# Opening of the first (gated linear attention) mixer: order of its first projections, their PSUM banks, and the zero matmuls

## What is computed

```python
def gla_mixer(h, w_in, w_gk2, b_gk, g_norm, w_out):
    proj = h @ w_in
    q, k, v, r, lr = jnp.split(proj, [GLA_DK, 2 * GLA_DK, 2 * GLA_DK + GLA_DV, 2 * GLA_DK + 2 * GLA_DV], axis=-1)
    gk = jax.nn.log_sigmoid((lr @ w_gk2 + b_gk).astype(f32)) / GLA_GATE_NORMALIZER
    ...
    b = jnp.cumsum(gc, axis=2)
    b_mid = b[:, :, GLA_CHUNK // 2:GLA_CHUNK // 2 + 1]
    q_in = qc * jnp.exp(b - b_mid)
    k_in = kc * jnp.exp(b_mid - b)
    causal = jnp.tril(jnp.ones((GLA_CHUNK, GLA_CHUNK), dtype=bool))
    scores = jnp.einsum('bcihd,bcjhd->bchij', q_in, k_in)
    ...
    o = rmsnorm(o, g_norm.reshape(GLA_HEADS, GLA_HV)).reshape(bsz, t_len, GLA_DV)
    o = o.astype(h.dtype) * jax.nn.silu(r)
    return o @ w_out
```

## Time and profile before

| | us |
|---|---|
| median of 3 runs | 1169.73 |
| lowest and highest | 1167.99, 1170.42 |
| the profiled execution, its own time | 1166.21 |
| its span in the trace | 1164.5 |
| TensorE busy in the span | 1111.0 (95%) |
| VectorE busy | 733.4 (63%) |
| ScalarE busy | 631.9 (54%) |
| TensorE's share of the chain that ended last | 88% |

### The profile page before, as it was taken

One profiled execution on the slowest core, in us unless ns is written; L12 is line 12 of the kernel. 1 busy time (PEld: TensorE's weight loads), 2 busy tenths in 40 slices (PEclk: granted clock), 3 DMA queues, 4 the chain that ended last, 5 costly groups with the idle time before them and its releaser, 6 DMA issues.

```text
span 1164.5 us, 16442 instructions
## 1 busy us (share of the span) xinstructions
PE 1111.0 (95%) x5868; PEld 947.5 (81%) x5868; DVE 733.4 (63%) x1170; ACT 631.9 (54%) x984; POOL 54.1 (5%) x81
## 2 busy tenths in 40 slices
PE   6899999969989999999999997999999989999997
PEld 5788888868968888888888885889999977888886
DVE  4555545656587555457655545598999978655553
ACT  6444444665367444447544444576776776544443
POOL 3000000000000000000000000221122100000000
PEclk9899999989999999999999999899999989999999
DMA  7756554444446565554756534484555424765530
GB/s 249 253 181 211 172 173 129 127 145 145 145 142 226 192 215 176 171 195 129 246 185 210 173 100 148 134 283 148 160 160 164 145 72 159 258 216 180 172 116 37
DMA packets 162877, 199.24 MB, mean 171 GB/s; under 512 B 6372, under 2 KB 145856, under 8 KB 162832
## 3 DMA queue, kind: packets, MB, share of 16 engines
q1 hardware_dynamic: 160144, 190.34, 50.4%
q0 software_dynamic: 2384, 7.72, 1.9%
q10 hardware_dynamic: 304, 0.61, 0.1%
HBM read 197.56 MB, written 1.08 MB: 171 GB/s over the span
## 4 chain that ended last, share of the span: by engine, by line
PE 88%; DVE 6%; ACT 3%; issue 1%; DMA 1%; SPq 0%; DVEq 0%; ACTq 0%
PE ps L1414 41%; PE ps L1433 25%; PE ps L1466 8%; PE ps L1476 6%; PE ps L1425 2%; PE ps L1775 1%; DVE ws L918 1%; DVE ws L1000 1%; PE ps L1456 1%; ACT ws L530 1%; DMA raw<-in_ffn_w_down 1%; PE ps L1584 1%; DVE xT L990 1%; DVE xres L966 0%; DVE ca L1191 0%
## 5 line engine op out<-in xcount | busy, mean ns | idle before, releaser
L1414 PE MATMUL ps<-ws,xT 128*128 128x512 f32 x2160 | 502.4, 391 | 6.2 <-DVE ws L1000 6.2
L1414 PEld LDWEIGHTS ps<-ws,xT 128*128 128x128 f32 x2160 | 404.9, 188 | 93.7 <-DVE ws L1000 8.0
L1433 PE MATMUL ps<-ws,hT 128*128 128x512 f32 x1344 | 335.2, 400 | 4.0 <-DVE hT L1291 3.9
L1433 PEld LDWEIGHTS ps<-ws,hT 128*128 128x128 f32 x1344 | 251.5, 191 | 57.5 <-issue 5.9
L1000 DVE TENSOR_TENSOR ws<-raw,ws 128x1024 fp32r<-128x1024 f32 x180 | 218.2, 1223 | 115.8 <-ACT ws L590 115.8
L918 DVE TENSOR_TENSOR ws<-raw,ws 128x2048 fp32r<-128x2048 f32 x90 | 206.4, 2293 | 98.1 <-ACT ws L530 97.7
L590 ACT ACTIVATE ws<-raw 128x1024 fp32r<-128x1024 f32 x180 | 188.4, 1061 | 144.9 <-PE ps L1414 139.8
L530 ACT ACTIVATE ws<-raw 128x2048 fp32r<-128x2048 f32 x90 | 171.0, 1913 | 62.7 <-PE ps L1433 57.1
L1466 PE MATMUL ps<-xT,ws 128*128 128x256 f32 x960 | 119.3, 284 | 0.3 <-ACT feat L536 0.3
L1466 PEld LDWEIGHTS ps<-xT,ws 128*128 128x128 f32 x960 | 116.4, 192 | 0.9 <-issue 0.9
L1476 PE MATMUL ps<-ws,xT 128*128 128x256 f32 x672 | 88.3, 292 | 0.4 <-ACT ca L536 0.3
(11 more groups left out here) (211 smaller groups left out, 613.0 us busy)
## 6 DMA issues: line engine op xcount, KB each, us to landing
raw<-in_ffn_w_down SPq DMA_DIRECT2D x88, 512.0 KB, 4.4
raw<-in_ffn_w_gate SPq DMA_DIRECT2D x86, 512.0 KB, 4.0
raw<-in_ffn_w_up SPq DMA_DIRECT2D x86, 512.0 KB, 5.0
raw<-in_ssd_w_in SPq DMA_DIRECT2D x48, 512.0 KB, 4.7
raw<-in_gla_w_in SPq DMA_DIRECT2D x24, 512.0 KB, 4.7
raw<-in_ssd_w_out SPq DMA_DIRECT2D x16, 512.0 KB, 4.5
raw<-in_gla_w_out SPq DMA_DIRECT2D x8, 512.0 KB, 4.7
exps<-cs_rows POOLq DMA_DIRECT2D x8, 512.0 KB, 8.5
```

Of the source, the lines that this page charges most:

```text
L1414: mm = pe.matmul(ps[:, bank + t, :].rearrange("p (s n) -> p s n", s=2), xT[:, k, a, t * P:(t + 1) * P], ws[:, 0:2, b, k * UW:(k + 1) * UW] ...
L1433: mm = pe.matmul(ps[:, 2 * t + n, :], hT[:, par, j, a, t * P:(t + 1) * P], ws[:, slot, b, off:off + 512], start=(first and j + a + b == 0) ...
```

## The change

On TensorE, `r_row` moves between the halves of the first pair, the `w_gk2` products stand right behind the pair, and head 0's queries and keys follow in one piece. In `body(1)` head 1's r goes to banks 0 and 1 and ahead of `rows(0)`; the zeros are gone, and head 0's contribution to the sum starts banks 0 to 3 itself; head 1's values go to banks 2 and 3, the first half between the state product and the output products. On DVE, head 1's P1 low part moves behind the steps up to `gla_dve` 1, the first four decayed products wait each for its own exponential and not all for the last, and the low part of head 2's P1 comes behind the copy of the state. On ACT the logarithm comes before the copies of head 0's queries and keys, the high part of head 1's values stands there too, and the high part of `w_out` (slot 3) goes to the end of `body(1)`. The loop of one turn is written out. No arithmetic is added.

```diff
@@ pipeline
-    with eng.Fori(2, n - 1) as g:
-        body(g, True, True, True)
+    if n == GLA_H:
+        for g in range(2, n - 1):
+            body(g, True, True, True)
+    else:
+        with eng.Fori(2, n - 1) as g:
+            body(g, True, True, True)
@@ ACT gla_start
-                tiles_out(SLOT_P3, n0[SLOT_P3], 2, [ca[:, c, :] for c in range(2)], p1_out)
                 act.wait_ge(gla_act, 1)
                 act.activation(et, et, ACT.Ln, bias=1.0).then_inc(gla_act, 1)
+                tiles_out(SLOT_P3, n0[SLOT_P3], 2, [ca[:, c, :] for c in range(2)], p1_out)
+                hi(SLOT_P3, n0[SLOT_P3] + 1)
@@ ACT mixer body
                     if proj:
-                        hi(SLOT_P3, g + n0[SLOT_P3])
-                        tiles_out(SLOT_P2, g + n0[SLOT_P2], A,
+                        if paired_first:
+                            act.wait_ge(zs_done, 1)
+                        else:
+                            hi(SLOT_P3, g + n0[SLOT_P3])
+                        tiles_out(SLOT_P2, g + n0[SLOT_P2], 0 if paired_first else A,
...
-                    if scan:
+                    if scan and not paired_first:
                         hi(*out_unit(g - 1, n, n0))
...
+                    if paired_first:
+                        hi(*out_unit(g - 1, n, n0))
@@ DVE gla_start
-                lo(SLOT_P1, n0[SLOT_P1] + 1)
                 dve.wait_ge(xT_lo, 32)
...
                 dve.scalar_tensor_tensor(out=et, in0=z, scalar=-1.0, in1=z, op0=ALU.mult, op1=ALU.max).then_inc(gla_dve, 1)
+                lo(SLOT_P1, n0[SLOT_P1] + 1)
                 lo(SLOT_P2, n0[SLOT_P2] + 1)
...
-                dve.wait_ge(gla_act, 7)
-                decayed(0, 0, (2, 0, 1, 3))
+                for o, exponentials in ((2, 4), (0, 5), (1, 6), (3, 7)):
+                    dve.wait_ge(gla_act, exponentials)
+                    decayed(0, 0, (o,))
@@ DVE mixer body
-                    if proj and not ahead:
+                    if proj and not ahead and not paired_first:
                         lo(SLOT_P1, g + n0[SLOT_P1] + 1)
...
+                    if paired_first:
+                        lo(SLOT_P1, g + n0[SLOT_P1] + 1)
@@ PE gla_start
                     small(GLA_RANK, ph)
+                    pe.wait_ge(r_done, NT * ph + 2)
+                    for t in range(NT):
+                        mm = pe.transpose(ps[0:GLA_RANK, E, t * P:(t + 1) * P], RPRE[t].broadcast_to([P, GLA_RANK]), ident[:, :])
+                    mm.then_inc(r_row, 1)
                 first_pair(ph, low_rank)
...
-                feature_tiles(SLOT_P3, 2, (0,))
...
                 mm.then_inc(gla_mm, 1)
-                feature_tiles(SLOT_P3, 2, (1,))
+                split(SLOT_P3, n0[SLOT_P3])
+                pe.wait_ge(post_read, 4 * ph)
+                feature_tiles(SLOT_P3, 2)
@@ PE mixer body
+                        opens = not ssd and o == 0
+                        if opens:
+                            pe.wait_ge(p3_out, 4)
                         for t in tiles:
-                            down_half(slot, par, t, 0, last=last)
+                            down_half(slot, par, t, 0, first=opens, last=last)
...
+                    if paired_first:
+                        split(SLOT_P2, g + n0[SLOT_P2])
+                        pe.wait_ge(p2_out, 2)
+                        pe.wait_ge(p3_out, 2)
+                        token_tiles(SLOT_P2, 0)
...
-                        if first and not ssd:
-                            open_banks()
...
+                        if paired_first:
+                            split(SLOT_P3, g + n0[SLOT_P3])
+                            token_tiles(SLOT_P3, 2, (0,))
+                            pe.wait_ge(w_done, 2)
+                            pe.wait_ge(p1_out, c0 + 2)
...
+                    elif paired_first:
+                        token_tiles(SLOT_P3, 2, (1,))
```

More of the change, by code:

```diff
@@ L39 @@
 SSD_WEIGHTS = 4
-SSD_STEPS, GLA_STEPS = 15, 17
+SSD_STEPS = 15
 MASKED_FIRST = 2
@@ L786, in body @@
                     first = isinstance(g, int) and g == 1
+                    paired_first = first and not ssd
                     ahead = isinstance(g, int) and g == n - 1
@@ L1383, in mixer @@
                 body(1, True, True, False)
-                per = SSD_STEPS if ssd else GLA_STEPS
-                with dve.Fori(2, n - 1) as g:
-                    step.body(g, 2, per)
-                    body(g, True, True, True)
-                step.after(n - 3, per)
+                if ssd:
+                    with dve.Fori(2, n - 1) as g:
+                        step.body(g, 2, SSD_STEPS)
+                        body(g, True, True, True)
+                    step.after(n - 3, SSD_STEPS)
+                else:
+                    for g in range(2, n - 1):
+                        body(g, True, True, True)
                 body(n - 1, True, True, True)
@@ L1728, in body @@
                         rows(g - 1)
-                    if proj:
+                    if proj and not paired_first:
                         split(SLOT_P2, g + n0[SLOT_P2])
@@ L1754, in body @@
                             pe.wait_ge(e_out, g)
-                        if not ssd:
+                        if not ssd and not paired_first:
                             pe.wait_ge(w_done, 2 * (g - 1 + G) + 2)
```

11 lines of the change are left out of this document (3 added, 8 removed).

## The result

| | before | changed |
|---|---|---|
| median, us | 1168.86 (4 runs, 1167.63 to 1170.42) | 1150.89 (4 runs, 1148.35 to 1153.55) |
| ratio to before | 1 | 0.9846, 95% interval 0.9819 to 0.9872 |
| profiled execution, us | 1166.21 | 1150.44 |
| its span, us | 1164.5 | 1148.7 |
| its mean granted clock | 0.979 | 0.985 |

The profiled executions, one of each kernel, lie 15.8 us apart.

What follows compares the result with a forecast made beforehand. The prediction took a chain through three engines to bound the mixer's opening; 11.22 us of idle time, 2.03 of lowered clock, 1.02 of zeros and about half a us at seams gave 14.75, so 1169.73 - 14.75 = 1155.0, range 1152 to 1160.

Steps and rivals of the forecast that it cites:

- The bound and the wait: Mixer's opening: a chain through three engines bounds it; TensorE's 9.0 us wait and three small waits (0.62, 1.33, 0.31) go.
- The layout: TensorE from the first pair's end to head 2's first projection: work sums to 28.29 us, 14.75 less than before.
- The chain: DVE and ACT decay steps: last exponentials start near 239.8, last product at 244.6, ahead of the transpose at 246.4.
- P1's low part: Head 1's P1 on DVE, moved behind the chain's steps: ready at 234.0, wanted by TensorE at 234.5, half a us spare.
- head 2's start: Head 0's gated output and the norm come in time for TensorE, 0.5 to 1 us spare each; cost 0.
- To spare: Margins before TensorE waits: 0.5 to 1.8 us at the transpose, 0.5 to 1 at each place of head 2's start.
- The clock at the gap: Behind the 9 us idle time, head 1's r ran at a lowered clock, 7.97 against 5.94 us: 2.03 us saved.
- The rule weighed: ACT's table switches: the skill page's 1380 ns drain would make the chain 2.7 us later; the profile row says 0.
- How the numbers follow: Whole kernel: 14.75 us subtracted from the profiled 1166.21 and the median 1169.73, giving 1151.5 and 1155.0.
- Rival (c): After the mixer, loads for the next feed-forward or head 3 give time back: saving 4 to 9 us, 1163; chance 0.05.
- the supply of weights: Rival that head 2's loads, issued 2.3 us later, come too late: slower, 1172 to 1175; chance 0.02.
- more saved than 15.3 us: Whole kernel: a saving above the forecast's 14 to 15.3 us; chance 0.01.

Runs made afterwards that it cites:

- e10: Changed kernel with all four first decayed products waiting for the last exponential again, as before; 1152.44 us (1 run), opening 34.12 us.
- e9: Changed kernel with two unused additions put into DVE's chain ahead of the sum along the tokens, 1.7 us longer; 1154.01 us (1 run), opening 34.94 us.
- e6: Changed kernel with the high part of head 1's values put back on ACT behind the copy of the decayed keys; 1159.14 us, ratio 0.9936 to before.
- e8: Kernel before with its 9 us idle gap filled by 72 unused matmuls on the normed input; 1165.69 us, ratio 0.9980 to before.
- e1: Changed kernel measured once more against before, nothing else altered; 1149.48 us, ratio 0.9853 to before.
- e4: Kernel with the changed mixer start, but head 0's and head 1's TensorE work in the old order and banks, with zeros; 1164.16 us, ratio 0.9972 to before.
- e13: Changed kernel with zero matmuls in fifteen idle places of TensorE outside the change; 1141.65 us, ratio 0.9773 to before.
- e14: Kernel before with the same fills as e13, its 9 us opening gap left empty; 1154.97 us, ratio 0.9891 to before.
- e11: Changed kernel with 124 unused matmuls (14.9 us) inserted between head 1's r and the transpose of head 0's decayed keys; 1169.18 us, ratio 1.0006 to before.
- e15: e13 with the 124 unused matmuls (14.9 us) of e11 inserted in the opening; 1156.31 us, ratio 0.9900 to before.
- e16: Changed kernel with 62 unused matmuls (7.4 us) inserted in the opening, seams not filled; 1161.68 us, ratio 0.9938 to before.
- e2: Kernel before with 30 matmuls of zeros put into the idle time ahead of the transpose of head 0's decayed keys; 1166.49 us, ratio 0.9996 to before.

## Why the prediction was right and wrong

*The bound and the wait: right.* The 9.0 us wait of the earlier trace rows is gone, with the three small ones and the fall of the clock of the earlier trace rows.

*The layout: right to 0.6 us.* It had 28.29 us from the end of the pair; the trace has 254.77 - 227.10 = 27.67, and the pair's own end lies 0.2 further from the small product than before. The 96 features took 11.62 and not 11.87, the transpose 0.20 and not 0.47. The difference was worked out as 14.75 and is 15.19, 0.4 more.

*The chain: right to 0.3 us.* Exponentials from 240.05 (239.8 laid out), last product 244.85 (244.6), transpose 246.40 on the change's own axis, which starts 0.2 later. DVE and ACT did meet within a tenth. P1's low part was there in time, and head 2's start had no wait.

*To spare: two places were missed.* I gave 0.5 to 1 us at the two places of head 2's start and 0.5 to 1.8 at the transpose, which has 1.5. The values' low part behind the last product has 0.5 (e10 found it), and ACT's copy of the keys 0.2 (e9 found it). It cost nothing here. It would have, had the high part of the values not moved, 4.9 us (e6), which the prediction put down only as a piece of the chain's length.

*The clock at the gap: right,* 2.03 against 2.14 (e8), or 1.72 by the second trace of before.

*The rule weighed: the row was right.* The sum with a drain at each switch would have been 2.7 us worse in the chain; it was not.

*The step that failed is "How the numbers follow".* It carried the sum over to the whole program as if the rest took the same time: "the forecast is 1169.73 - 14.75". Two terms are wrong in it. First the base: 1169.73, the median of three, was high; the 23 runs of before beside e1 to e4 have 1167.24, and of all its 79 runs the mean is 1167.7, some 2.1 less. Secondly the stretch behind head 2 was given no term and no bound, though the trace of before could have said that it holds lowered clock too: over the whole span the mean is 0.979, and the prediction spoke of one window with 0.68. Over the changed kernel's eight runs (mean 1150.4) the saving on 1167.7 is 17.2, of which 15.0 are the opening (48.67 or 48.25 less 33.48) and 2.2 the seams. 2.1 + 0.3 + 2.2 are the 4.6 us by which 1155.0 was too high. The 2.2 are what is left of the times; the traces behind head 2 bear them out (894.8 and 896.9 before, 893.9 and 892.1 changed), and that this stretch's difference is the clock is e13 and e14. Rival (c) looked at that stretch for what it might give back, and not for what it might add.

*No rival came about.* Nothing was given back, the supply of weights did not matter. What came, more saved than 15.3 us, had been given a chance of 0.01; the opening alone, 14.8 to 15.2 less, lies inside the forecast's 14 to 15.3.

*Open.* Why the clock falls at one seam in one execution and not in the next, why the unshifted places are better ones, and how small a shift ends that, is not shown. That a shift of 7.4 or 14.9 us matters is (e11, e15, e16). How much the clock behind the gap costs in the usual execution of before is known from three traces only.

## What to carry to other kernels

A wait on a long chain is best removed from both ends: the chain pulled ahead and independent work put in front of the waiter; here the halves gave 3.3 and 5.3 us alone and 17 together, and one buffer's conversion on a third engine decided whether they met. When a piece moves, all later short waits of TensorE come at other times and may cost another clock: give that a term of its own, from the spread of the traces, or close them first. Closing them paid about half of what the change did: e13 is 1141.65 us, 0.9773 of before, 8 to 9 us below the changed kernel, with the same work otherwise.

## What the runs showed of the hardware

- A wait of 0.6 and one of 1.3 us with little work around them were enough for the granted clock to fall to half in one trace, and not in another (0.57 and 1.00 over the same 8 us). At this seam it fell for 3 to 7 us where it fell. The Trainium skill has such a case, "TensorE: Matmul & The Clock Gate", section "A second HAM failure mode: psum-queue depth-cycling", where short idle times between groups of matmuls cost a clock that swings. This case's traces agree that short idle times can do it, at 0 to 3 us for a seam; they show single falls and no steady swing.
- Matmuls of zeros hold the clock (e13, granted clock 0.998 to 0.999 over the whole kernel) as matmuls on data do (e8). No length of idle time that is safe comes out of it: 2.1 us behind 7 us of zeros were too much in e2, 2.1 behind 2.9 in e14, and 2.7 behind 2.9 at the same place in e13 were not. One matmul of zeros of 512 columns takes 0.23 us.
- A stretch of 886 us of work, with 16 us between two kernels' starts into it, repeats to 0.2 us in three traces (886.14, 886.14, 886.30) once its clock no longer falls.
- `ACT_TABLE_LOAD` between two activations takes 1.3 us from its start to the start of what follows and shows no drain, before and after the change (237.48 to 238.78, and 234.04 to 235.33).
